# Sums of weight blocks for the second feed-forward network: formed in SBUF on the way to TensorE, in place of sums kept in HBM

## The chip, the cores and the metric

One core of one Trainium2 chip. The time is device microseconds (us) of one execution. Before the change the kernel takes 1630.29 us, the median of 3 runs (1623.0 to 1633.59). The engines are TensorE (PE; its weight load is PEld), VectorE (DVE), ScalarE (ACT), GpSimd (POOL) and SyncE (SP), which only issues transfers. All five run their own instruction streams in program order and meet at semaphores.

## The reference, cut to what matters

One layer of a decoder for 512 prompt tokens and 32 new tokens (544 columns), model width 1024:

```python
h = h + 0.5 * _swiglu(_rms(h, g_ffn1), w_ffn1_gate, w_ffn1_up, w_ffn1_down)
mix, ... = _mixer(_rms(h, g_mix), ...)       # S5 branch and latent attention branch
h = h + mix
h = h + 0.5 * _swiglu(_rms(h, g_ffn2), w_ffn2_gate, w_ffn2_up, w_ffn2_down)
y = _rms(h, g_final)

def _swiglu(x, w_gate, w_up, w_down):        # gate, up: 1024 x 2816; down: 2816 x 1024
    return (silu(x @ w_gate) * (x @ w_up)) @ w_down
```

All inputs are float32. The change is in how the weights of the second `_swiglu` reach TensorE.

## The kernel before, in words

**Precision.** Each float32 operand is split in a high part (fp32r, a rounding, by ScalarE) and a low part (the rest, a subtraction, by VectorE). A product is three matmuls: hi x hi, hi x lo, lo x hi. So every weight block passes ScalarE and then VectorE before TensorE may use it.

**Order of the work.** First FFN (22 blocks of 128 hidden columns in groups of 6, 6, 6 and 4; per group 12 or 8 gate and up tiles of 48 matmuls, then 8 down tiles with 6 or 4 chunks, so 36 or 24 matmuls); then the projections of the mixer with the S5 scan; attention; output; the second FFN. In the first FFN `split_hi` (L750, ScalarE: w_hi<-raw) and `split_lo` (L1405, VectorE: w_lo<-raw,w_hi) run two tiles ahead of TensorE (`products`, L2126). GpSimd forms the hidden product (L1199, L1201), and between its groups the tables of the S5 branch (L1283 to L1317), which wait for VectorE's `s5_parameters`. Later GpSimd adds squares for the norms (`add_squares`, L1190: m_sum), clears hprev and multiplies ktrig (L1347). TensorE's column sums (L2140) wait for m_sum, and a product with ropesum (L2384) for ktrig.

**The second FFN** is computed by a scheme with seven products in place of eight for each 2 x 2 arrangement of blocks (Strassen and Winograd). A unit takes four blocks A11, A12, A21, A22 of a weight. For 20 of the 22 hidden blocks the gate and the up tile, each in two halves, are the four (a gate/up unit; blocks of 128 x 512); 12 units are of the down weight (128 x 384). The first two hidden blocks and the last part of the down weight are computed plainly. The seven products P1 to P7 of a unit have these weights: P1 A11, P2 A12, P4 A22, P5 S1 = A21 + A22, P6 S2 = A11 + S1, P7 S3 = A11 + A21, P3 S4 = A12 + S2. A product is 12 matmuls (gate/up) or 9 (down) of 272 columns, by `product` (L2233). `ORDER` interleaves neighbouring units: P1 n, P2 n, P3 n-1, P7 n, P6 n, P4 n-1, P5 n. `part_hi` (L864, ScalarE) and `part_lo` (L1514, VectorE) split the weight of product k+8 after product k (NWS = 8 places). In a gate/up unit ScalarE evacuates P1 (L923), P7 (L925), P6 (L927) and P3 (L929), VectorE P2, P5 and P4 (L1571, L1575, L1579); in a down unit VectorE adds all seven to h (L1548). TensorE's P5 waits for the evacuation of P6 (p6_out), its P3 and P4 for that of P5 (c22), since the banks are accumulated on.

**Where the sums come from.** S1 to S4 of all 32 units lie in HBM (s2_a, s2_d). They are made during the first FFN and the mixer: `weight_copies` (L808) lets ScalarE issue 36 copies from HBM to HBM, some after each down tile of the first FFN, right behind `split_hi` in its program. `weight_sums` lets GpSimd issue 36 transfers that add in HBM, in three steps (L1245, then L1239, then L1234), each behind a wait for the step before. Its six calls stand between the pieces of GpSimd's work named above, two of them behind `add_squares(N_Q)` and `add_squares(N_KV)`; the third stands ahead of the hprev clearing and `add_squares(N_Q)`, and the fourth ahead of ktrig. In the second FFN SyncE loads one block per product, P1 to P7 of each unit (L736, a ring of 11 places wr).

**The hidden product** of a pair of blocks has seven combinations for the down units. GpSimd multiplies silu and up (L1262) and forms four sums (L1270, L1272 to L1274: hv<-hv). ScalarE (`hidden_hi`, L878 and L879: h_hi) and VectorE (`hidden_lo`, L1536: h_lo) split them after the product k in `READY`: for seven pairs that is a P3 of a gate/up unit, for two a P4 of a down unit.

## Time and profile before

| | us |
|---|---|
| median of 3 runs | 1630.29 |
| profiled execution, time | 1638.77 |
| its span | 1636.8 |
| PE busy (82%) | 1345.1 |
| DVE busy (46%) | 759.1 |
| ACT busy (31%) | 508.7 |
| POOL busy (24%) | 389.8 |

The profile shows one execution. Lines as L808 are those of the kernel's code. Instructions that issue transfers aren't counted as busy; where a transfer's issue holds an engine, its next instruction has "issue" as the end of its idle time. ACTq, POOLq and SPq are the engines' sequencers. PEclk is the clock that TensorE was granted, as a share of 2.4 GHz (0.5 is the lower level, 1.2 GHz). The trace has the transfers of the second FFN as wr<-w_gu, wr<-s_a, wr<-s_d and wr<-w_d2a or w_d2b, the copies as s_a<-w_gu and s_d<-w_d2a or w_d2b on ACTq, and the additions on POOLq. In the stretch 1382 to 1444 us gate/up units run, in 1444.8 to 1476 us down units. A few matmul records can be missing.

### The profile page before, as it was taken

Reading aid. Unit: us, or ns where it says so; the run is one execution under the profiler, and the core shown is the slowest. Engines: PE = TensorE matmul, PEld = TensorE weight load, DVE = VectorE, ACT = ScalarE, POOL = GpSimd, SP = SyncE. Lnnn points to the kernel's source line nnn. Section 1 sums busy time; section 2 is a strip of 40 time slices with the busy share of each in tenths; the row PEclk is TensorE's granted clock in tenths of the full one; section 3 lists DMA queues with packets and bytes.
Section 4 is the critical chain, followed back from the end, with each engine's and each line's share of the span. In section 5 each row is a group of like instructions: output and inputs, shape, how many; then the busy total and the mean of one; then the engine's idle time right before and its main releaser. Section 6 shows DMA issues by size and latency. Waiting matters only on the chain.

```text
span 1636.8 us, 28404 instructions
## 1 busy us (share of the span) xinstructions
PE 1345.1 (82%) x11292; PEld 1235.8 (76%) x11292; DVE 759.1 (46%) x1301; ACT 508.7 (31%) x941; POOL 389.8 (24%) x401
## 2 busy tenths in 40 slices
PE   7965389747973884819489999998999699999998
PEld 7964389747973884819376777765999699999997
DVE  6322033402220232629153444454556877686774
ACT  5220032002210221201023333243334564655554
POOL 0216013602280111211135222220121231221202
PEclk9986689968986896859788999999999899999998
DMA  6222232446266534858467999997523356556541
GB/s 214 76 83 85 105 126 83 141 105 165 80 168 139 156 104 179 207 108 189 85 175 240 318 340 335 347 321 288 184 87 97 110 158 198 170 171 187 148 150 55
DMA packets 157799, 273.26 MB, mean 167 GB/s; under 512 B 42161, under 2 KB 65106, under 8 KB 155506
## 3 DMA queue, kind: packets, MB, share of 16 engines
q1 hardware_dynamic: 96802, 199.72, 37.2%
q0 software_dynamic: 41344, 34.84, 11.6%
q10 hardware_dynamic: 19536, 37.10, 6.0%
q8 instruction: 79, 1.29, 0.3%
q14 instruction: 38, 0.31, 0.1%
HBM read 261.69 MB, written 70.50 MB: 203 GB/s over the span
## 4 chain that ended last, share of the span: by engine, by line
PE 51%; issue 17%; ACTq 11%; DVE 6%; DMA 6%; POOL 4%; ACT 3%; SPq 1%; another core or an unknown queue 1%; DVEq 0%; POOLq 0%
PE d L2126 20%; ACTq L808 11%; PE d L2233 8%; PE e L2233 8%; PE e L2471 5%; DMA kv<-kv_src 2%; DMA s_a<-w_gu 2%; DVE w_lo L1405 2%; ACT w_hi L750 2%; PE e L2503 1%; DMA raw<-w_q 1%; PE e L2522 1%; PE d L2535 1%; POOL s_a L1245 1%; SPq L538 1%
## 5 line engine op out<-in xcount | busy, mean ns | idle before, releaser
L1405 DVE TENSOR_TENSOR w_lo<-raw,w_hi 128x1024 fp32r<-128x1024 f32 (+2 forms) x127 | 152.6, 1201 | 443.7 <-ACT w_hi L750 443.4
L2126 PE MATMUL d<-x_hi,w_hi 128*128 128x272 f32 x976 | 216.2, 304 | 129.3 <-DVE w_lo L1405 75.8
L2126 PEld LDWEIGHTS d<-x_hi,w_hi 128*128 128x128 f32 x976 | 163.5, 201 | 135.4 <-DVE w_lo L1405 78.5
L750 ACT CAST w_hi<-raw 128x1024 fp32r<-128x1024 f32 (+2 forms) x127 | 123.3, 971 | 450.2 <-issue 213.2
L2126 PE MATMUL d<-x_lo,w_hi 128*128 128x272 f32 x976 | 210.7, 299 | 0.0
L2126 PE MATMUL d<-x_hi,w_lo 128*128 128x272 f32 x976 | 210.6, 299 | 0.0
L1514 DVE TENSOR_TENSOR ws_lo<-wr,ws_hi 128x512 fp32r<-128x512 f32 (+1 forms) x224 | 158.8, 711 | 68.4 <-ACT ws_hi L864 66.2
L2126 PEld LDWEIGHTS d<-x_lo,w_hi 128*128 128x128 f32 x976 | 162.8, 200 | 0.0
L2126 PEld LDWEIGHTS d<-x_hi,w_lo 128*128 128x128 f32 x976 | 161.8, 200 | 0.0
L864 ACT CAST ws_hi<-wr 128x512 fp32r<-128x512 f32 (+1 forms) x224 | 129.8, 581 | 85.5 <-PE d L2233 44.5
L2126 PE MATMUL d<-hid_hi,w_hi 128*128 128x272 f32 x352 | 83.4, 322 | 67.2 <-DVE w_lo L1405 66.0
L2126 PEld LDWEIGHTS d<-hid_hi,w_hi 128*128 128x128 f32 x352 | 62.8, 215 | 72.1 <-DVE w_lo L1405 35.2
L1381 POOL DMA_INDIRECT kr<-kr_src,gidx x64 | 60.9, 952 | 176.1 <-PE e L2506 165.2
L1262 POOL TENSOR_TENSOR hv<-sl,upb 128x544 f32<-128x544 f32 x21 | 36.1, 1718 | 259.3 <-DVE upb L1579 195.1
L2233 PE MATMUL e<-x_hi,ws_hi 128*128 128x272 f32 x280 | 82.2, 293 | 13.2 <-DVE ws_lo L1514 6.9
L1199 POOL TENSOR_TENSOR hid<-silu,up 128x544 f32<-128x544 f32 x21 | 31.0, 1475 | 235.6 <-DVE up L1466 235.6
L2233 PE MATMUL e<-x_hi,ws_lo 128*128 128x272 f32 x280 | 82.0, 293 | 0.0
L2233 PE MATMUL d<-x_hi,ws_hi 128*128 128x272 f32 x280 | 81.8, 292 | 0.0
L2233 PE MATMUL d<-x_hi,ws_lo 128*128 128x272 f32 x280 | 81.8, 292 | 0.0
L2233 PE MATMUL e<-x_lo,ws_hi 128*128 128x272 f32 x280 | 81.6, 292 | 0.0
L2233 PE MATMUL d<-x_lo,ws_hi 128*128 128x272 f32 x280 | 81.5, 291 | 0.0
L2126 PE MATMUL d<-hid_lo,w_hi 128*128 128x272 f32 x352 | 79.3, 310 | 0.0
(435 smaller groups left out, 3176.7 us busy)
## 6 DMA issues: line engine op xcount, KB each, us to landing
kv<-kv_src SPq DMA_DIRECT2D x256, 256.0 KB
raw<-w_gu SPq DMA_DIRECT2D x47, 512.0 KB, 5.8
wr<-s_a SPq DMA_DIRECT2D x80, 256.0 KB, 2.8
raw<-w_post SPq DMA_DIRECT2D x34, 512.0 KB, 4.4
...
wr<-w_gu SPq DMA_DIRECT2D x60, 256.0 KB, 3.0
...
```

Source lines behind the costliest of these rows:

```text
L538: sp.dma_start(dst, src).then_inc(s, 16)
L750: nc.scalar.copy(w_hi[:, s % 2, 0:n, :], raw[:, raw_pos(s), 0:n, :]).then_inc(S.hi_done, 1)
L808: nc.scalar.dma_start(summed(kind, q, i0, i1), weight_block(kind, QUARTER[q], i0, i1)).then_inc(sem["cp%d" % g], 16)
L864: nc.scalar.copy(ws_hi[k % NWS][:, 0:n, :], wr[k % NWR][:, 0:n, :]).then_inc(S.w_hid, 1)
L1199: nc.gpsimd.tensor_tensor(hid[:, j, :], silu[:, j, :], up[:, j, :], ALU.mult).then_inc(S.hid_done, 1)
L1262: nc.gpsimd.tensor_tensor(hv[:, 1:3, :] if j % 2 else hv[:, 0:8:7, :], halves(sl[:, j % 2, :]), halves(upb[:, j % 2, :]), ALU.mult).then_i ...
L1381: nc.gpsimd.indirect_dma_start(kr[v % NKR][:, j, :], None, a["kr_src"], bass.IndirectOffsetOnAxis(ap=gidx32[:, n:n + 1].bitcast(U32), axis ...
L1405: nc.vector.tensor_tensor(w_lo[:, s % 2, 0:n, :], raw[:, raw_pos(s), 0:n, :], w_hi[:, s % 2, 0:n, :].bitcast(FP), ALU.subtract).then_inc(S ...
L1514: nc.vector.tensor_tensor(ws_lo[k % NWS][:, 0:n, :], wr[k % NWR][:, 0:n, :], ws_hi[k % NWS][:, 0:n, :].bitcast(FP), ALU.subtract).then_inc ...
L2126: ins = mm(out[:, b, :], w[:, pos, c0 + k, :], x[:, k, b * HALF:(b + 1) * HALF], start=first, stop=stop)
L2233: ins = mm(out, w[k % NWS][:, c, :], v, start=typ in ("P1", "P2", "P7") and c == 0 and w is ws_hi and v is xh, stop=c == steps(n) - 1 and ...
L2471: ins = mm(job_bank(k), w[:, s % 2, c0 + c, :], x[:, c, half], start=c == 0 and x is xh and w is w_hi, stop=c == nk - 1 and w is w_lo)
```

## The change

The sums no longer exist in HBM. `weight_copies`, `weight_sums`, s2_a and s2_d are gone, and with them SyncE's wait for sums3. SyncE loads four blocks per unit, A11, A12, A21 and A22, 128 loads for 224, in a ring of 8 places: four for even units and four for odd. The load of a block for unit n waits until its last reader in unit n-2 is done. The sums are made in place in the loaded blocks, one after the other, each after the split that reads the place has finished:

- GpSimd, for all units: A11 += A21 (S3, after P1's split), A21 += A22 (S1).
- For gate/up units VectorE, right after the low part of P7's and of P6's weight: A11 += A22 (S2), A11 += A12 (S4). For down units GpSimd makes these two.
- ScalarE's split of P7, P5, P6 and P3 waits for the sum it reads.

GpSimd's order in the second FFN is now: sums of unit n+1, then the product silu x up of unit n-1's block. The four sums of each pair of hidden blocks (`hidden_sums`) move to VectorE, after `part_lo` and ahead of `hidden_lo` at the places in `READY`; `hidden_hi` waits for them as before.

```diff
-    NWR, NWS = 11, 8
+    NWR, NWS = 8, 8
...
+    HELD = ("A11", "A12", "A21", "A22")
+    FROM = {"P1": "A11", "P2": "A12", "P7": "A11", "P6": "A11", "P3": "A11", "P4": "A22", "P5": "A21"}
+    READ = {"A11": (0, 0), "A12": (0, 1), "A22": (1, 1), "A21": (1, 0)}
...
+    def read_last(n, x):
+
+        if x == "A12":
+            return S.s4_sum, n + 1
+        return after("w_lod", AT[{"A11": "P3", "A22": "P4", "A21": "P5"}[x], n] + 1)
...
-        sp.wait_ge(S.sums3, 16 * sum(len(g) for g in GROUPS))
-        for k in range(NP + KC):
-            if 3 <= k < NWR:
-                sp.wait_ge(S.lo_done, S_FFN2 + (k - 3) // 2 + 1)
-            if k >= NWR:
-                sp.wait_ge(*after("w_lod", k - NWR + 1))
-            if k >= NP:
-                src, n = a["w_d2b"][k - NP, :, (BLOCKS[1] + BLOCKS[2]) * P:], NLAST
-            else:
-                typ, u_ = ORDER[k]
-                src, n = unit_source(u_, typ), steps(u_)
-            sp.dma_start(wr[k % NWR][:, 0:n, :], src.rearrange("p (c n) -> p c n", n=P)).then_inc(sem[WR_IN[k % NWR][0]], 16)
+        def weight_load(n, x):
+
+            if n >= 2:
+                sp.wait_ge(*read_last(n - 2, x))
+            elif held(n, x) >= 3:
+                sp.wait_ge(S.lo_done, S_FFN2 + (held(n, x) - 3) // 2 + 1)
+            sp.dma_start(wide(n, x), weight_block(n, *READ[x]).rearrange("p (c n) -> p c n", n=P)).then_inc(sem[WR_IN[held(n, x)][0]], 16)
+
+        when = {"A12": 4.5, "A21": 6.5, "A11": 9.5, "A22": 12.5}
+        for n in range(2):
+            for x in ("A11", "A12", "A21", "A22"):
+                weight_load(n, x)
+        for t, n, x in sorted((7 * n + when[x], n, x) for n in range(2, NU) for x in HELD):
+            weight_load(n, x)
+        for m in range(KC):
...
+            typ, n = ORDER[k]
+            x = FROM[typ]
+            if typ == "P6":
+                act.wait_ge(S.s2_sum, n + 1)
+            elif typ == "P3":
+                act.wait_ge(S.s4_sum, n + 1)
+            elif typ == "P7":
+                act.wait_ge(S.s3_sum, n + 1)
+            elif typ == "P5":
+                act.wait_ge(S.s1_sum, n + 1)
+            else:
+                act.wait_ge(*landed(n, x))
...
-        def weight_sums(step):
-
-            if 0 <= step - 2 < len(GROUPS):
-                pool.wait_ge(S.sums2, 16 * sum(len(g) for g in GROUPS[:step - 1]))
-                for kind, i0, i1 in GROUPS[step - 2]:
-                    pool.dma_start(long_rows(summed(kind, 4, i0, i1)), long_rows(summed(kind, 2, i0, i1)), accum_op=ALU.add,
-                                   max_dma_last_dim=8192).then_inc(S.sums3, 16)
-            if 0 <= step - 1 < len(GROUPS):
-                pool.wait_ge(S.sums1, 32 * sum(len(g) for g in GROUPS[:step]))
-                for kind, i0, i1 in GROUPS[step - 1]:
-                    pool.dma_start(long_rows(summed(kind, 2, i0, i1)), long_rows(summed(kind, 1, i0, i1)), accum_op=ALU.add,
-                                   max_dma_last_dim=8192).then_inc(S.sums2, 16)
-            if step < len(GROUPS):
-                pool.wait_ge(sem["cp%d" % step], 64 * len(GROUPS[step]))
-                for kind, i0, i1 in GROUPS[step]:
-                    for q, x in ADDED.items():
-                        pool.dma_start(summed(kind, q, i0, i1), weight_block(kind, x, i0, i1), accum_op=ALU.add,
-                                       max_dma_last_dim=8192).then_inc(S.sums1, 16)
...
+        def add_in_place(n, to, x, done):
+
+            pool.wait_ge(*landed(n, x))
+            nc.gpsimd.tensor_tensor(wide(n, to), wide(n, to), wide(n, x), ALU.add).then_inc(done, 1)
...
-                pool.wait_ge(*after("mul", j + 1))
-                if j == 0:
-                    pool.wait_ge(*after("x7l", 3))
-                if j % 2 == 0:
-                    nc.gpsimd.tensor_tensor(hv[:, 3, :], hv[:, 0, :], hv[:, 7, :], ALU.subtract)
-                else:
-                    link(nc.gpsimd.tensor_tensor(hv[:, 5, :], hv[:, 7, :], hv[:, 2, :], ALU.subtract))
-                    link(nc.gpsimd.tensor_tensor(hv[:, 4, :], hv[:, 5, :], hv[:, 0, :], ALU.subtract))
-                    nc.gpsimd.tensor_tensor(hv[:, 6, :], hv[:, 1, :], hv[:, 4, :], ALU.add).then_inc(S.hvt, 1)
-
-            for j in range(sum(BLOCKS) - 1):
-                hidden(j, None)
+
+            for n in range(-1, NU):
+                if n + 1 < NU:
+                    pool.wait_ge(*after("w_lod", AT["P1", n + 1] + 1))
+                    add_in_place(n + 1, "A11", "A21", S.s3_sum)
+                    pool.wait_ge(S.s3_sum, n + 2)
+                    add_in_place(n + 1, "A21", "A22", S.s1_sum)
+                    if dense(n + 1):
+                        pool.wait_ge(*after("w_lod", AT["P7", n + 1] + 1))
+                        add_in_place(n + 1, "A11", "A22", S.s2_sum)
+                        pool.wait_ge(*after("w_lod", AT["P6", n + 1] + 1))
+                        add_in_place(n + 1, "A11", "A12", S.s4_sum)
+                if n + 2 <= HEAD:
+                    hidden(n + 1)
+                if n >= 1 and not dense(n - 1):
+                    hidden(pair_of(n - 1))
...
+            if typ == "P7" and not dense(n):
+                add_in_place(n, "A22", k, S.s2_sum)
+            if typ == "P6" and not dense(n):
+                add_in_place(n, "A12", k, S.s4_sum)
+
+        def add_in_place(n, x, k, done):
+
+            dve.wait_ge(*after("w_lod", k + 1))
+            dve.wait_ge(*landed(n, x))
+            nc.vector.tensor_tensor(wide(n, "A11"), wide(n, "A11"), wide(n, x), ALU.add).then_inc(done, 1)
...
+        def hidden_sums(q):
+            dve.wait_ge(*after("mul", 2 * q + 2))
+            nc.vector.tensor_tensor(hv[:, 3, :], hv[:, 0, :], hv[:, 7, :], ALU.subtract)
+            link(nc.vector.tensor_tensor(hv[:, 5, :], hv[:, 7, :], hv[:, 2, :], ALU.subtract))
+            link(nc.vector.tensor_tensor(hv[:, 4, :], hv[:, 5, :], hv[:, 0, :], ALU.subtract))
+            nc.vector.tensor_tensor(hv[:, 6, :], hv[:, 1, :], hv[:, 4, :], ALU.add).then_inc(S.hvt, 1)
...
                 if k in READY:
+                    hidden_sums(READY[k])
                     hidden_lo(READY[k])
```

## Rows read from the trace of the kernel before

**Rows 1.** The page's part 2: TensorE's busy tenths in forty slices
```profile
PE   7965389747973884819489999998999699999998
```

**Rows 2.** Stretches: length; busy (count) PE, PEld, DVE, ACT, POOL; clock, DMA, GB/s
```profile
103.80:210.20 106.40, 42.67 (x242) 41.36 (x241) 19.50 (x50) 9.43 (x13) 27.69 (x86) 0.69 0.26 92
319.40:392.00 72.60, 30.75 (x194) 30.09 (x193) 9.07 (x9) 6.40 (x8) 10.76 (x7) 0.71 0.48 118
473.20:546.40 73.20, 30.78 (x170) 29.83 (x169) 9.91 (x11) 4.86 (x6) 14.17 (x12) 0.67 0.63 149
602.50:660.50 58.00, 24.12 (x116) 22.88 (x115) 14.23 (x17) 11.53 (x18) 6.98 (x6) 0.67 0.46 167
698.40:731.40 33.00, 0.09 (x2) 0.06 (x1) 3.92 (x7) 1.59 (x2) 4.97 (x5) 0.54 0.46 92
779.60:800.70 21.10, 0.04 (x2) 0.01 (x1) 4.36 (x6) 1.04 (x1) 3.24 (x2) 0.58 0.58 105
838.40:845.40 7.00, 0.17 (x2) 0.08 (x1) 0.61 (x1) 1.48 (x3) 0.75 (x1) 0.70 0.82 243
```

**Rows 3.** Chain that ended last: start us, length us, what
```profile
30.84 54.37 PE d L2126 x432
...
1292.81 3.06 PE e L2233 x12
1295.87 4.27 PE d L2233 x24
```

**Rows 4.** Line 808: ns min/median/max, first and last start
```profile
L808 ACTq DMA_DIRECT2D s_a<-w_gu x24: 1214/10982/26296, 92.6 to 649.1; - x24
```

**Rows 5.** Waits, 97 to 212 us: total us, times, longest
```profile
ACT w_hi L750 <- issue: 71.8, 4, 21.5
```

**Rows 6.** Instructions in order of time, GpSimd, 583 to 880 us
```profile
725.60 1.88 POOL L1245 DMA_DIRECT2D s_a<-w_gu  x1 [44.12 <-issue]
```

**Rows 7.** Waits, 700 to 800 and 800 to 872 us
```profile
PE e L2140 <- POOL m_sum L1190: 32.9, 1, 32.9
...
PE e L2384 <- POOL ktrig L1347: 21.1, 1, 21.1
```

**Rows 8.** Busy time by stretch: gate and up units, then down units
```profile
1382.00:1444.00 62.00, 62.00 (x496) 61.99 (x495) 43.88 (x67) 38.89 (x77) 15.18 (x12) 1.00 0.55 164
1444.80:1476.00 31.20, 31.20 (x251) 31.20 (x250) 26.32 (x54) 14.59 (x28) 6.94 (x6) 1.00 0.66 196
```

**Rows 9.** Groups of instructions by shape, 1250 to 1637 us; busy us, mean ns
```profile
L1514 DVE TENSOR_TENSOR ws_lo<-wr,ws_hi 128x512 fp32r<-128x512 f32 x140 | 104.9, 753 | 51.7 <-ACT ws_hi L864 49.6
L1514 DVE TENSOR_TENSOR ws_lo<-wr,ws_hi 128x384 fp32r<-128x384 f32 x84 | 53.9, 641 | 16.7 <-ACT ws_hi L864 16.6
...
L1579 DVE TENSOR_TENSOR upb<-d,upb 128x272 f32<-128x272 f32 x10 | 4.4, 435 | 1.0 <-PE d L2233 1.0
...
L1262 POOL TENSOR_TENSOR hv<-sl,upb 128x544 f32<-128x544 f32 x21 | 36.1, 1718 | 259.3 <-DVE upb L1579 195.1 <-issue 42.0 <-DVE upb L1587 22.3
L1270 POOL TENSOR_TENSOR hv<-hv 128x272 f32<-128x272 f32 x9 | 9.7, 1076 | 10.7 <-DVE x_lo L1521 10.1
```

**Rows 10.** In order of time, ScalarE, around one P3 of the second FFN
```profile
1417.76 0.40 ACT L929 ACTIVATE sl<-e 128x272 f32<-128x272 f32 x1 [0.81 <-PE e L2233]
...
1418.57 0.88 ACT L878 CAST h_hi<-hv 128x816 fp32r<-128x816 f32 x1
1419.34 1.10 ACT L879 CAST h_hi<-hv 128x1088 fp32r<-128x1088 f32 x1
...
1421.47 0.38 ACT L927 COPY upb<-d 128x272 f32<-128x272 f32 x1
```

**Rows 11.** DMA issues: count, KB each, median us to landing
```profile
wr<-w_gu SPq DMA_DIRECT2D x60, 256.0 KB, 3.0
```

**Rows 12.** In order of time, VectorE: alone, then beside GpSimd
```profile
1423.43 0.68 DVE L1514 TENSOR_TENSOR ws_lo<-wr,ws_hi 128x512 fp32r<-128x512 f32 x1
...
1424.54 1.34 DVE L1514 TENSOR_TENSOR ws_lo<-wr,ws_hi 128x512 fp32r<-128x512 f32 x1
```

More of the change, by code:

```diff
@@ L328, in tile_of, with weight_block, held, wide @@
         return j if b + 1 == NB else j0 + (j - j0) // 2 + nb // 2 * ((j - j0) % 2)
-    SUMMED = [t for t in range(sum(BLOCKS)) if t not in [tile_of(j) for j in range(HEAD)]]
-    assert SUMMED == [1, 2] + list(range(4, 22)) and BLOCKS == (6, 6, 6, 4)
-    DB = KC // 2
-    GROUPS = ((("g", 0, 2), ("g", 2, 4), ("g", 4, 8)), (("d", 0, 4), ("g", 8, 12)), (("d", 4, 8), ("g", 12, 16)), (("d", 8, 12), ("g", 16, 20)))
-    QUARTER = {1: 2, 2: 0, 3: 0, 4: 1}
-    ADDED = {1: 3, 3: 2}
-    def weight_block(kind, x, i0, i1):
-        row, half = divmod(x, 2)
+    HELD = ("A11", "A12", "A21", "A22")
+    FROM = {"P1": "A11", "P2": "A12", "P7": "A11", "P6": "A11", "P3": "A11", "P4": "A22", "P5": "A21"}
+    READ = {"A11": (0, 0), "A12": (0, 1), "A22": (1, 1), "A21": (1, 0)}
+    def weight_block(n, row, half):
+        kind, where = UNITS2[n]
         if kind == "g":
-            t0, t1 = SUMMED[i0], SUMMED[i1 - 1] + 1
-            assert t1 - t0 == i1 - i0
-            return a["w_gu2"][2 * t0 + row:2 * t1 + row - 1:2, :, half * KC // 2 * P:(half + 1) * KC // 2 * P]
-        b, i = divmod(i0, DB)
+            return a["w_gu2"][2 * tile_of(where) + row][:, half * KC // 2 * P:(half + 1) * KC // 2 * P]
+        b, i = where
         w = BLOCKS[0] // 2 * P
         src, c = (a["w_d2a"], half * w) if b == 0 else (a["w_d2b"], (2 * (b - 1) + half) * w)
-        i1 -= b * DB
-        return src[2 * i + row:2 * i1 + row - 1:2, :, c:c + w]
-    def summed(kind, q, i0, i1):
-        return (s2_a if kind == "g" else s2_d)[q - 1, i0:i1]
-    def unit_source(n, typ):
-        x, kind = SOURCE[typ], UNITS2[n][0]
-        i = SUMMED.index(tile_of(pair_of(n))) if kind == "g" else DB * pair_of(n)[0] + pair_of(n)[1]
-        return (weight_block(kind, x, i, i + 1) if x < 4 else summed(kind, x - 3, i, i + 1))[0]
+        return src[2 * i + row][:, c:c + w]
+    def held(n, x):
+        return NWR // 2 * (n % 2) + HELD.index(x)
+    def wide(n, x):
+        return wr[held(n, x)][:, 0:steps(n), :]
+    def landed(n, x):
+        name, first = WR_IN[held(n, x)]
+        return sem[name], first + 16 * (n // 2 + 1)
+    def last_held(m):
+        i = (NWR // 2 * (NU % 2) + m) % NWR
+        n = NU + (i // (NWR // 2) != NU % 2)
+        return i, n, HELD[i % (NWR // 2)]
     def dense(n):
@@ L512, in build @@
                  trig_done uk_in hprev_zero gp_out0 gp_out1 gp_evac cqs_done qn_done zn_done gate_done merged_done mh_done m_ready fin_diag fin_rep gain_done y_dve dve_own pool_own
-                 cp0 cp1 cp2 cp3 sums1 sums2 sums3 p6_out p7_out""".split())
+                 s1_sum s3_sum s2_sum s4_sum p6_out p7_out""".split())
     sem = {n: nc.alloc_semaphore(n) for n in sem_names}
@@ L528, in build @@
              [("x_in%d" % i, 16) for i in range(4)] +
-             [("raw_in%d" % i, 16 * raw_count(S_FFN2 + i)) for i in range(NRAW)])
+             [("raw_in%d" % i, 16 * raw_count(S_FFN2 + i)) for i in range(NWR - NKV - 4)])
     S = type("Sems", (), sem)
@@ L802, in last_down @@
             last_root(1)
-        def weight_copies(g, m):
-            copies = [(kind, q, i0, i1) for kind, i0, i1 in GROUPS[g] for q in (1, 3, 2, 4)]
-            for kind, q, i0, i1 in copies[m * len(copies) // KC:(m + 1) * len(copies) // KC]:
-                nc.scalar.dma_start(summed(kind, q, i0, i1), weight_block(kind, QUARTER[q], i0, i1)).then_inc(sem["cp%d" % g], 16)
         def ffn(norm, g_next, norm_next):
@@ L862, in part_hi @@
                 act.wait_ge(S.tile_done, T_FFN2 + 3 + (k >= 6))
-            n = steps(ORDER[k][1])
-            nc.scalar.copy(ws_hi[k % NWS][:, 0:n, :], wr[k % NWR][:, 0:n, :]).then_inc(S.w_hid, 1)
+            nc.scalar.copy(ws_hi[k % NWS][:, 0:steps(n), :], wide(n, x)).then_inc(S.w_hid, 1)
         def x7_split_hi(i):
```

33 lines of the change are left out of this document (11 added, 22 removed).

## The prediction

> **What bounds the kernel now.** I read the page's forty slices first. TensorE is busy in nine tenths or more of nearly all slices from the twenty-second on (860 us), but in one to five tenths of several before, as in the fourth, fifth and eighteenth [rows 1]. So the span has two parts with different limits. I then cut the first part at the places where TensorE stands still. Seven stretches come out [rows 2]: together 371.3 us long, with only 728 matmuls in them. The price of one matmul without a stall is 54.37/432 = 0.126 us [rows 3], so these stretches hold 728 x 0.126 = 92 us of TensorE work and 279 us of something else. The granted clock in them is 0.54 to 0.71, a mixture of the 1.2 and the 2.4 GHz level.
>
> What is the something else? In the first stretch ScalarE's weight split (w_hi, L750) waits 71.8 us for "issue", that is, for its own queue [rows 5]. What stands in that queue is L808: each copy of a weight block from HBM to HBM holds ScalarE for a median of 10.98 us, up to 26.3 us, though nothing is computed [rows 4]. VectorE's half of the split waits for ScalarE's, TensorE for VectorE's. Stretches two to four have the same shape. Stretches five and six are GpSimd's: it issues the accumulating transfers (L1245) and is idle 44.12 us ahead of one [rows 6]; behind it in program order stand the additions m_sum and the product ktrig, for which TensorE waits 32.9 and 21.1 us [rows 7]. The seventh (7 us) is a late load of w_q, at a DMA share of 0.82 [rows 2].
>
> The second FFN, from about 1265 us, is the other kind: 62.00 of 62.00 us busy where gate and up units run, 31.20 of 31.20 where down units run, clock 1.00 [rows 8]. TensorE is the bound there and nothing can be gained; whatever the change adds there is either hidden or lost.
>
> **The change, part by part.**
>
> *1. Removed: 36 copies on ScalarE, 36 accumulating transfers on GpSimd.* What each stretch gives back is its length less its matmuls at 0.126 us [rows 2, 3]: 106.4 - 30.5 = 76; 72.6 - 24.4 = 48; 73.2 - 21.4 = 52; 58.0 - 14.6 = 43; 33.0; 21.1; 7.0 (7 at most). I don't take all of it, since something else is late next. In stretch four ScalarE and VectorE each have some 2.9 us of their own work per tile (w, x, h, square) against 24 x 0.126 = 3.0 us of TensorE, and the last x_lo, then m_sum, come one after the other: I leave 5 us there. In stretch five VectorE would still have its scan work, which now hides in the wait: 3 us left. One us each stays in six and seven. The S5 tables on GpSimd and VectorE, and the loads, run at another time than now but fit beside the tiles: GpSimd is busy 27.7 us of the 106 in the first stretch, mostly with the tables, and its next product is due only after four down and two gate/up tiles, 240 matmuls or 30 us of TensorE. Sum: 76 + 48 + 52 + 38 + 30 + 20 + 6 = 270 us.
>
> *2. Clock restarts.* After a gap the matmuls start at the lower level: twelve took 3.06 us after the gap at 1288 to 1293 us, where 1.51 would be full pace, and the next 24 took 4.27 us for 3.02 [rows 3]. That is 2.8 us behind one gap. The work behind six of the seven stretches starts so, outside the windows; at about 2 us each: 12 us. Parts 1 and 2: **282 us** less, bounds 230 (clock and half of what I left at nothing stay) and 295.
>
> *3. SyncE.* 224 loads become 128 of the same size; there is no wait for sums3, which is over long before. A load takes 3.0 us to land [rows 11]. The tightest block, A11, is free again after P3's split and wanted five products later, at least 5 x 9 x 0.126 = 5.7 us. Cost nothing; if transfers took twice as long, the first product of a unit would wait some 1 us, 30 times.
>
> *4. Additions in SBUF.* GpSimd gets 2 for each of 20 gate/up units and 4 for each of 12 down units, VectorE 2 for each of the 20. Nothing in the trace is this very instruction; the nearest are VectorE's two-input subtractions of the same size, 0.753 us (512) and 0.641 (384), and GpSimd's 1.718 us for 544 columns [rows 9]. So VectorE's addition is about 0.75 and GpSimd's about 1.6 us for 512 and 1.2 for 384; as bounds 0.68 to 1.34 (the same subtraction took 1.34 us beside GpSimd [rows 12]). GpSimd's load is 40 x 1.6 + 48 x 1.2 = 122 us over 306: it has the room. VectorE: 43.88/62 of a 10.6 us unit is 7.5 us now; plus 2 x 0.75, plus the moved sums (4 x 0.435 per two units [rows 9]) makes 9.9 of 10.6. It fits, with 7% to spare.
>
> GpSimd against VectorE: in 272 columns the trace has 1.076 against 0.435 us [rows 9]. The Trainium skill, *GPSIMD Engine Reference*, § 4.1 Engine selection, speaks against this part of the change: it gives elementwise work on a tile to VectorE, GpSimd being about twice as slow with two inputs; § 1 adds that the two share an SBUF interface. By that rule the 88 additions would go to VectorE, 40 x 0.75 + 48 x 0.64 = 61 us more of its time, which its 7% to spare doesn't hold; by the rows they lie beside TensorE's work on GpSimd, and only the slowdown of VectorE costs. The ratio agrees (2.5 here), the advice does not follow for an engine with nothing else to do.
>
> *5. The new waits.* The splits now hang on the additions: P7's on GpSimd's, P6's and P3's on one behind the previous split. They run eight products ahead, which absorbs that. But ScalarE and VectorE run in order, and behind a waiting split stands the evacuation of the product that TensorE needs soon: P5 waits for p6_out, one product after P6. In a down unit P6's split waits for a subtraction (0.56), GpSimd's sum (1.2) and then takes 1.1 itself: p6_out comes some 0.5 to 1 us late. Nine such units: 7 us. In a gate unit VectorE makes the sum in 0.75 us and the slack holds.
>
> *6. The sums of the hidden product* (36 instructions, four per pair) go from GpSimd to VectorE, behind the split and its addition. Now, in one such place, ScalarE starts h_hi at 1418.57, 0.8 us after P3 is done, because the sums were ready; it ends at 1420.4, and p6_out (L927) is written at 1421.8 [rows 10]. P5 could start at 1417.7 + 3 x 1.51 = 1422.2: 0.4 us of slack. In the new order VectorE finishes P7's subtraction about 1.7 us after P3, the addition at 2.4, the four sums at 2.4 + 4 x 0.45 = 4.2; only then h_hi (1.9), p7_out, P6's split, silu and p6_out (1.5): 7.6 us after P3, where 4.5 was free. **3.1 us of stall, seven times = 22 us**; the two pairs whose sums come behind a down unit's P4 lose about 2 us each through c22 (4 us). A gap of 3 us also brings the clock down (2.8 us by [rows 3] for a 5 us gap, nothing if the gap is too short): at 1.5 each, 13 us. Between ends of 0 (the waits overlap something) and 9 x 6 = 54 I take 39.
>
> *7. Start of the second FFN:* VectorE is the bound of those 25 us; two additions and one wait more: 4 us.
>
> Loss in the second FFN: 7 + 39 + 4 = **50 us**, bounds 10 and 110. The sum is against the profiled execution (span 1636.8, time 1638.77 us): 1638.8 - 282 + 50 = 1407. The median of the three runs is 8.5 us below that execution; taken off, 1398. I say **1400 us**.
>
> **Rivals.** (a) *The second FFN hides everything*: for it speaks that splits run eight products ahead; against it the 0.4 us of slack. 1630 - 282 + 0 to 10 = 1350. Chance 0.14.
> (b) *VectorE becomes the second FFN's bound*: 9.9 of 10.6 us on average leaves no room for contention; if every subtraction and addition takes the 0.95 us that lies between 0.68 and 1.34, a gate unit takes 7 x 0.25 + 2 x 0.25 = 2.2 us more, so 12.1 for 10.6, and a down unit 26.32/31.20 x 7.9 = 6.7 now, plus 7 x 0.2 of contention and 1.4 of waiting, 9.5 for 7.9: 20 x 1.5 + 12 x 1.6 = 49 us, on top of parts 6 and 7: about 1445 to 1490. For it: the 1.34 us row. Against: GpSimd loses 4 us of its own sums per pair. Chance 0.14.
> (c) *GpSimd's stretches stay*: the chain behind m_sum and ktrig is VectorE's scan and not the transfers, and stretches four to seven keep their length. Only 76 + 48 + 52 + 6 = 182 come back: 1630 - 182 + 50 = 1498. Against it: GpSimd was idle for 44 us with "issue" in front. Chance 0.07.
> (d) *Slower than before*: the stalls of the second FFN come so regularly that TensorE stays at 1.2 GHz there. 2436 matmuls at 0.255 us (3.06/12) take 621 us for 307: +314, against -282: 1630 - 282 + 314 = 1662. It decides against the change only if the clock is below 307/(307 + 282) = 0.52 through the whole FFN; the worst stretch now, with gaps of 5 to 15 us, has 0.54. Chance 0.02.
> (e) *The change doesn't do what it says*, the first part being slowed by something that stays: near 1630 plus the loss or minus a little. Chance 0.02.
>
> **The numbers.** The forecast has 0.61 with its own range 1365 to 1450. Taking in (a) at 1350 and the near part of (b) gives 1345 to 1470, with about 0.2 outside. One per cent, 16 us, is about what a measurement of this kernel tells from no change. Faster by over 1%: all but (d) and (e), 0.96; within 1%: 0.02; slower: 0.02.
>
> **What would show it.** In the profile after: no L808 and no L1245; the second FFN's products starting some 280 us earlier; ScalarE's "issue" wait ahead of w_hi gone; no TensorE gap over 5 us between there and the start. In the second FFN: seven gaps near 3 us in front of P5 (ScalarE h_hi waiting for VectorE's hv), two of 2 us in front of P3; GpSimd busy 150 us or more. The prediction is wrong if TensorE has no such gaps (a), if VectorE is at 95% there and TensorE's gaps are spread over all units (b), or if the m_sum wait stays above 10 us (c).

## The result: 1402 us for 1630, and the profile after

The changed kernel takes 1402.0 us (median of 4 runs, 1395.5 to 1408.2), the kernel before 1630.1 (1623.0 to 1633.6): ratio 0.8605, 95% interval [0.8557, 0.8654]. The forecast was 1400, range 1345 to 1470. The profiled execution of the changed kernel has a span of 1399.8 us.

The page of the profile after, part 2, answers to [rows 1]: TensorE's busy tenths and its granted clock, each slice now 35 us.

```profile
PE   7999999999999999999999989997698888898987
...
PEclk9999999999999999999999999999799999999999
```

The first part of the span has no slice below nine after the first; the holes have moved behind slice 28. The view by stretch shows both ends. Cut at the column sums of the norms, after (from, to, length; busy us and count of PE, PEld, DVE, ACT, POOL; clock, DMA share, GB/s):

```profile
22.00:435.20 413.20, 408.31 (x3519) 403.64 (x3518) 172.12 (x235) 117.83 (x148) 160.04 (x192) 1.00 0.28 87
435.20:471.00 35.80, 35.80 (x372) 34.92 (x373) 27.61 (x37) 8.21 (x10) 3.70 (x3) 1.00 0.35 116
471.00:540.20 69.20, 68.68 (x859) 63.25 (x858) 55.43 (x103) 13.58 (x17) 6.17 (x2) 1.00 0.24 75
540.20:946.00 405.80, 396.46 (x3650) 310.78 (x3650) 207.45 (x446) 146.28 (x341) 100.50 (x95) 1.00 0.73 256
946.00:1399.80 453.80, 379.93 (x2813) 373.35 (x2812) 354.58 (x541) 207.14 (x404) 153.79 (x121) 0.93 0.23 74
```

and the last two of these stretches before the change:

```profile
826.00:1250.40 424.40, 406.52 (x3651) 318.25 (x3650) 207.93 (x446) 146.58 (x341) 101.20 (x97) 0.97 0.75 258
1250.40:1636.80 386.40, 360.81 (x2813) 358.77 (x2812) 282.14 (x465) 209.74 (x404) 81.92 (x69) 0.97 0.48 145
```

Before, the third cut stood at 826.0; now it stands at 540.2: 286 us came back. In the attention part (fourth row) 18.6 us came back: 9.8 by the first ukt product, which is the seventh stretch of [rows 2] and its restart; the rest is the clock (1.00 for 0.97) in code that the change doesn't touch. The second feed-forward network (FFN) gave 67.4 us away, 453.8 for 386.4. Length less busy time is TensorE's idle time: 73.9 for 25.6, so 48.3 us more; its busy time is 19.1 us more, since matmuls behind a gap run at the lower clock. 286 + 18.6 - 67.4 = 237 = 1636.8 - 1399.8.

What the idle time waited for: the waits of the changed kernel, 990 to 1372 us (engine line, awaited: total us, times, longest).

```profile
ACT h_hi L892 <- DVE hv L1539: 28.5, 9, 3.5
ACT ws_hi L878 <- POOL wr L1239: 22.3, 9, 3.0
...
PE d L2243 <- ACT upb L941: 18.1, 7, 3.3
```

The first row has nine waits of ScalarE's h_hi for the moved sums; behind seven of them TensorE's P5 waits for p6_out (L941, third row). The second row is ScalarE's weight split waiting for GpSimd's sums. One such place in order of time (start, us, ..., idle before), the answer to [rows 10]; ScalarE:

```profile
1026.88 0.40 ACT L943 ACTIVATE sl<-e 128x272 f32<-128x272 f32 x1 [0.81 <-PE e L2243]
1027.18 0.61 ACT L878 CAST ws_hi<-wr 128x512 fp32r<-128x512 f32 x1
1031.00 0.87 ACT L892 CAST h_hi<-hv 128x816 fp32r<-128x816 f32 x1 [3.21 <-DVE hv L1539]
1031.78 1.09 ACT L893 CAST h_hi<-hv 128x1088 fp32r<-128x1088 f32 x1
1032.78 0.38 ACT L939 COPY upb<-d 128x272 f32<-128x272 f32 x1
1033.05 0.62 ACT L878 CAST ws_hi<-wr 128x512 fp32r<-128x512 f32 x1
1033.57 0.43 ACT L905 ACTIVATE sl<-sl 128x272 f32<-128x272 f32 x1
1033.90 0.37 ACT L941 COPY upb<-d 128x272 f32<-128x272 f32 x1
```

VectorE:

```profile
1023.09 1.21 DVE L1506 TENSOR_TENSOR ws_lo<-wr,ws_hi 128x512 fp32r<-128x512 f32 x1 [0.25 <-ACT ws_hi L878]
1024.87 1.34 DVE L1506 TENSOR_TENSOR ws_lo<-wr,ws_hi 128x512 fp32r<-128x512 f32 x1 [0.57 <-ACT ws_hi L878]
1026.13 0.42 DVE L1580 TENSOR_TENSOR sl<-sl,d 128x272 f32<-128x272 f32 x1
1026.48 2.10 DVE L1506 TENSOR_TENSOR ws_lo<-wr,ws_hi 128x512 fp32r<-128x512 f32 x2
1028.62 0.69 DVE L1517 TENSOR_TENSOR wr<-wr,wr 128x512 f32<-128x512 f32 x1
1029.23 0.43 DVE L1536 TENSOR_TENSOR hv<-hv 128x272 f32<-128x272 f32 x1
```

and TensorE's P5, after 3.05 us:

```profile
1034.42 0.36 PE L2243 MATMUL d<-x_hi,ws_hi 128*128 128x272 f32 x1 [3.05 <-ACT upb L941]
```

This is the chain that the prediction wrote out: split, addition, four sums, h_hi, p7_out, P6's split, silu, p6_out. Two of the four subtractions of weights (L1506) among VectorE's rows took 1.21 and 1.34 us, where one alone takes 0.68; both lie beside GpSimd's two-input instructions. The groups of instructions after, which answer to [rows 9]:

```profile
L1506 DVE TENSOR_TENSOR ws_lo<-wr,ws_hi 128x512 fp32r<-128x512 f32 (+1 forms) x224 | 193.6, 868 | 53.0 <-ACT ws_hi L878 51.3
L1239 POOL TENSOR_TENSOR wr<-wr,wr 128x384 f32<-128x384 f32 (+1 forms) x88 | 110.7, 1259 | 163.5 <-DVE ws_lo L1506 155.3
```

VectorE's subtractions (L1506) take 868 ns in the mean, where the kernel before had 711.

### The profile page after: what moved, and what is told of

Read it like the earlier page. It is cut to its first block, busy times and chain, and to the rows that moved or that the text cites. A ratio compares the mean times of both kernels' runs of the same rounds, so it can differ in the third digit from the quotient of the medians.

```text
span 1399.8 us, 28490 instructions
## 1 busy us (share of the span) xinstructions
PE 1303.8 (93%) x11292; PEld 1200.2 (86%) x11292; DVE 829.8 (59%) x1377; ACT 507.0 (36%) x941; POOL 424.5 (30%) x417
## 4 chain that ended last, share of the span: by engine, by line
PE 70%; DVE 10%; issue 6%; DMA 4%; POOL 4%; ACT 3%; SPq 1%; ACTq 0%; POOLq 0%; DVEq 0%
PE d L2136 36%; PE d L2243 7%; PE e L2243 7%; PE e L2481 6%; DMA kv<-kv_src 3%; DVE ws_lo L1506 2%; POOL wr L1239 2%; PE e L2513 2%; DVE w_lo L1397 2%; PE e L2532 1%; PE d L2545 1%; SPq L541 1%; ACT ws_hi L878 1%; PE e L2516 1%; PE d L2566 1%
## 5 line engine op out<-in xcount | busy, mean ns | idle before, releaser
L1506 DVE TENSOR_TENSOR ws_lo<-wr,ws_hi 128x512 fp32r<-128x512 f32 (+1 forms) x224 | 193.6, 868 | 53.0 <-ACT ws_hi L878 51.3
L2136 PE MATMUL d<-x_hi,w_hi 128*128 128x272 f32 x976 | 205.2, 292 | 10.5 <-DVE w_lo L1743 6.8
L2136 PE MATMUL d<-x_lo,w_hi 128*128 128x272 f32 x976 | 202.4, 289 | 0.0
L2136 PEld LDWEIGHTS d<-x_hi,w_hi 128*128 128x128 f32 x976 | 154.7, 190 | 13.2 <-DVE w_lo L1743 6.8
L1239 POOL TENSOR_TENSOR wr<-wr,wr 128x384 f32<-128x384 f32 (+1 forms) x88 | 110.7, 1259 | 163.5 <-DVE ws_lo L1506 155.3
L2136 PEld LDWEIGHTS d<-x_lo,w_hi 128*128 128x128 f32 x976 | 154.6, 190 | 0.0
L2136 PEld LDWEIGHTS d<-x_hi,w_lo 128*128 128x128 f32 x976 | 153.6, 190 | 0.0
L2136 PE MATMUL d<-hid_hi,w_hi 128*128 128x272 f32 x352 | 74.4, 292 | 4.1 <-DVE w_lo L1397 2.7
L2243 PEld LDWEIGHTS e<-x_hi,ws_hi 128*128 128x128 f32 x280 | 57.2, 204 | 22.9 <-DVE ws_lo L1506 16.3
L2243 PEld LDWEIGHTS d<-x_hi,ws_hi 128*128 128x128 f32 x280 | 56.0, 200 | 22.7 <-issue 22.7
```

The source lines that it names most:

```text
L1239: nc.gpsimd.tensor_tensor(wide(n, to), wide(n, to), wide(n, x), ALU.add).then_inc(done, 1)
L1506: nc.vector.tensor_tensor(ws_lo[k % NWS][:, 0:steps(n), :], wide(n, FROM[typ]), ws_hi[k % NWS][:, 0:steps(n), :].bitcast(FP), ALU.subtract ...
L2136: ins = mm(out[:, b, :], w[:, pos, c0 + k, :], x[:, k, b * HALF:(b + 1) * HALF], start=first, stop=stop)
L2243: ins = mm(out, w[k % NWS][:, c, :], v, start=typ in ("P1", "P2", "P7") and c == 0 and w is ws_hi and v is xh, stop=c == steps(n) - 1 and ...
```

## The experiments

Theory at the start (**order**): TensorE's gaps come from what stands in program order ahead of p6_out on ScalarE and VectorE; move it, and they go. Rival (**work**): VectorE has too much to do, by number of instructions or because GpSimd's additions stretch them. For each kernel the second FFN is cut as above, from its column sums to the end:

| kernel | time, us | ratio to before, 95% | FFN 2 | PE idle | PE busy | DVE busy |
|---|---|---|---|---|---|---|
| before | 1630.1 | 1 | 386.4 | 25.6 | 360.8 | 282.1 |
| f_none | 1341.6 | 0.8205 [0.8172, 0.8239] | 386.7 | 25.4 | 361.3 | 282.4 |
| f_copies | 1509.7 | 0.9238 [0.9201, 0.9275] | 386.3 | 25.4 | 360.9 | 282.3 |
| changed kernel | 1402.0 | 0.8605 [0.8557, 0.8654] | 453.8 | 73.9 | 379.9 | 354.6 |
| s_gpsimd | 1399.4 | 0.8569 [0.8534, 0.8605] | 440.6 | 68.5 | 372.1 | 344.5 |
| d_vector | 1404.6 | 0.8590 [0.8556, 0.8625] | 447.0 | 69.4 | 377.6 | 362.8 |
| s_early2 | 1394.3 | 0.8538 [0.8511, 0.8565] | 436.7 | 65.5 | 371.2 | 362.1 |
| s_early | 1393.9 | 0.8535 [0.8510, 0.8560] | 436.3 | 63.5 | 372.8 | 357.8 |
| d_defer | 1400.8 | 0.8584 [0.8557, 0.8611] | 444.4 | 66.8 | 377.6 | 358.9 |
| c_both2 | 1380.4 | 0.8460 [0.8435, 0.8485] | 428.3 | 52.5 | 375.8 | 358.1 |
| h_later | 1387.4 | 0.8487 [0.8466, 0.8508] | 429.2 | 54.6 | 374.6 | 361.1 |
| x_gp_small | 1379.8 | 0.8447 [0.8419, 0.8475] | 426.9 | 53.8 | 373.1 | 313.3 |
| v_only | 1402.1 | 0.8587 [0.8564, 0.8611] | 442.2 | 67.6 | 374.7 | 359.0 |
| v_all2 | 1364.8 | 0.8369 [0.8349, 0.8390] | 410.5 | 41.8 | 368.7 | 357.7 |

The stretches are those of one profiled execution each; PE idle varies least, since the clock's part falls differently from one execution to the next.

**f_none: the transfers out, nothing put in.** In the kernel before:

```diff
-                    weight_copies(b, m)
...
-        weight_sums(3)      # and the five other calls
...
-        sp.wait_ge(S.sums3, 16 * sum(len(g) for g in GROUPS))
...
-        return (weight_block(kind, x, i, i + 1) if x < 4 else summed(kind, x - 3, i, i + 1))[0]
+        return weight_block(kind, x % 4, i, i + 1)[0]
```

> The kernel before without the 36 copies and the 36 accumulating transfers, and without SyncE's wait for them; every one of the 224 loads of the second FFN takes an unsummed weight block of the same size, so the sums are left out and all else stays. Theory: the part ahead of the second FFN gives back what the changed kernel gave back there, 305 us by its traces, and the second FFN keeps its old length: 1630 - 305 = 1325 us (1315 to 1335), the second FFN's column sums at about 946 us, as in the changed kernel. By my forecast's own sum it would be 1630 - 282 = 1348. Rival (c), GpSimd's stretches belong to VectorE's scan: 1630 - 182 = 1448. Rival: part of the 305 us comes from the fewer loads of the changed kernel (128 for 224): above 1335.

Measured 1341.6 us. By stretch:

```profile
22.00:435.10 413.10, 408.32 (x3516) 403.45 (x3515) 172.54 (x235) 117.89 (x148) 159.73 (x191) 1.00 0.29 87
...
540.10:954.60 414.50, 402.04 (x3650) 314.53 (x3649) 207.56 (x446) 146.40 (x341) 100.59 (x95) 0.98 0.72 250
954.60:1341.30 386.70, 361.29 (x2814) 359.13 (x2812) 282.38 (x465) 209.74 (x404) 82.28 (x69) 0.97 0.48 145
```

The cuts lie where the changed kernel has them, within 0.1 us up to 540, and the second FFN has its old length. So the two halves of the change add up, and the number of loads (224 or 128) is nothing. The theory's range (1315 to 1335) was missed by 7 us, and above 1335 stood the rival that fewer loads gave a part. It isn't needed: f_none's attention part (414.5 us, with 224 loads still to come) lies in the middle of those of the ten experiments with 128. The whole gain of the front, by the ratio, is 0.1795 x 1634.6 = 293 us (288 to 299): more than the 282 of the forecast, less than the 305 that the two profiled executions show, because attention took 405.8 us in the one and 424.4 in the other; the twelve experiments have 409.5 to 419.0.

**f_copies: only GpSimd's transfers out.** As f_none, but `weight_copies` stays.

> The kernel before with ScalarE's 36 copies but without GpSimd's 36 accumulating transfers (the additions are left out; SyncE waits for the copies). Theory: the first three stretches stay, 76 + 48 + 52 = 176 us and their restarts; stretches five and six (30 + 20) and part of four (0 to 38) go, about 60 to 90 us: 1540 to 1570 us, the m_sum and ktrig waits of 32.9 and 21.1 us under 2 us. Rival: the copies are slow because the accumulating transfers fill the same DMA engines: then the copies' 10.98 us falls to under 6 us, the first three stretches shrink by half or more and the time is below 1480. Rival (c): 1620 or more, the two waits stay.

Measured 1509.7 us, below the theory's range and above the rival's. Waits over the whole execution, and the copies' line (ns min/median/max, first and last start), which answers to [rows 4]:

```profile
ACT w_hi L751 <- issue: 125.0, 11, 21.5
```

```profile
L809 ACTq DMA_DIRECT2D s_a<-w_gu x24: 1218/10137/16855, 92.5 to 587.2; - x24
```

The waits for m_sum and ktrig are gone, so rival (c) is out. The copies still hold ScalarE for 10.1 us at the median (10.98 before), but 16.9 at most, not 26.3; ScalarE's wait, 125.0 us in 11 times, was 213.2 us in 14 times before. The mixer's column sums start at 600.1 us: 62 us of what the prediction gave to the copies alone in stretches one to four came from copies that ran beside the accumulating transfers; 165 us (600.1 - 435.1) are the copies' own. The first stretch is unchanged, the second and third shrank.

**s_gpsimd: the sums of the pair back on GpSimd**, behind its product (the four instructions move from `hidden_sums` to `hidden`).

> The changed kernel with one part undone: the four sums of each hidden pair are GpSimd's again, right behind its product, ahead of its additions for the next unit. Theory (what counts is what stands in order in front of ScalarE's p6_out): h_hi no longer waits for VectorE, but GpSimd's additions come 4.3 us later and P7's split waits for S3 in its place, by some 2 us; the gaps shrink from 3.0 to about 2, nine times, 1385 to 1400 us. Rival (VectorE's amount of work is the bound, 2.6% of its time taken away): the gaps of the gate units go and also those of the down units get smaller, 1365 to 1380 us. Rival (the move cost nothing): 1402, gaps as now.

1399.4 us: no gain that the intervals tell. The nine gaps of 3 us went, but there are 17 gaps of 0.6 to 1.8 us now, two of 3.3, and the three of 2.5 to 2.8 at the transitions from down to gate units stay. The time lies at the upper end of the theory's range; the count of gaps fits neither theory.

**d_vector: S2 and S4 of the down units on VectorE.**

> The changed kernel with S2 and S4 of the 12 down units on VectorE, as in the gate/up units (24 additions of 384 columns moved from GpSimd). Theory: in a down unit P6's split waits for a subtraction and a sum; VectorE's sum takes about 0.6 us where GpSimd's takes 1.01 and has a semaphore more, so p6_out comes 0.5 us earlier and the seven gaps of 1.1 to 1.75 us shrink by about 0.5 each, 3 to 5 us in all: 1397 us. Rival (VectorE's amount of work is the bound): 24 x 0.6 us = 14 us more of its time makes gaps in the down units grow, 1405 to 1420 us.

1404.6 us, the same: above the theory's 1397, just under the rival's 1405. In the profile the down units' gaps (all of 0.4 us and more) fell from 11.0 to 6.3 us in all, close to what order says, and the time doesn't show it.

**s_early2 and s_early: the four sums two products, or one, ahead.**

```diff
+                if k + 2 in READY:          # s_early: k + 1
+                    hidden_sums(READY[k + 2])
                 if k in READY:
-                    hidden_sums(READY[k])
                     hidden_lo(READY[k])
```

> The changed kernel with VectorE's four sums of a hidden pair two products earlier in its program (behind the split after P1 in place of P3; for two pairs P7 in place of P4), where VectorE still had idle time; ScalarE's h_hi stays. Theory (order in front of p6_out): the nine gaps of 2.6 to 3.3 us fall under 0.6 us, 26 us, and with them some 12 us at the lower clock; the gaps of the down units stay. The second FFN, 453.8 us in the changed kernel from its column sums to the end, gets 415 to 422 us long: time 1402 - 35 = 1367 us (1360 to 1378). Rival (VectorE's amount of work is the bound): the work is the same, so the gaps move to the products ahead (P2, P3) and the time stays within 1395 to 1405.

> As the last, but one product earlier only (behind the split after P2; P6 for the two of P4). There VectorE works without a break, so the sums end 1.9 us earlier because the split of P7 and its addition now come behind them. Theory: the nine gaps of 3.0 us shrink by 1.9 to about 1.1, 17 us, and most of the clock's part goes: 1372 to 1385 us. Rival (amount of work): 1395 to 1405.

1394.3 and 1393.9: 8 us, at the edge of what the intervals tell, where 35 and 25 were expected. The order theory failed in its size. Nine gaps of 3 us became gaps of 0.9 to 1.8 in nearly every unit. VectorE works without a break from 1033 to 1040 us there, and the sums themselves are stretched: in s_early2, in order of time,

```profile
1032.67 1.62 POOL L1239 TENSOR_TENSOR wr<-wr,wr 128x512 f32<-128x512 f32 x1
1033.07 1.53 DVE L1536 TENSOR_TENSOR hv<-hv 128x272 f32<-128x272 f32 x1
```

0.43 us of work takes 1.53 beside GpSimd's addition.

**d_defer: P6's split behind the evacuation of the P6 before it.**

```diff
+    def one_later(part, k):
+        late = lambda i: i < NP and ORDER[i][0] == "P6"
+        if late(k + NWS - 1):
+            part(k + NWS - 1)
+        if not late(k + NWS):
+            part(k + NWS)
...
-                part_hi(k + NWS)            # part_lo the same
+                one_later(part_hi, k)
```

> The changed kernel with one step of ScalarE's and VectorE's order changed: the split of a P6 (high and low part, with VectorE's addition behind it) comes one product later in their programs, behind the evacuation of the P6 before it in place of ahead of it. Theory: the seven gaps of 1.1 to 1.8 us in the down units (10 us) and the three of 2.5 to 2.8 us where a down unit is followed by a gate/up unit (8 us) go, and the seven in front of P5 shrink by the split and the wait for its sum, 1.2 to 1.5 each (9 us); with 5 to 10 us of clock the second FFN gets 415 to 425 us long: 1366 us (1360 to 1382). Rival (amount of work): no gain in the down units, 1390 or more. Rival (the split of P6 gets late itself, since it has seven products of lead in place of eight): P6's own start shows a new gap.

1400.8 us, the same as the changed kernel. The down units' gaps went (0.7 to 0.9 left) and those of the three transitions fell from 2.5 to 2.8 to 1.7 or 1.8, but the nine others took 29 us in all for 26.5: four of them are 2.5 to 2.8 us long now, five 3.3 to 4.1. Why, in order of time:

```profile
1024.87 0.43 DVE L1596 TENSOR_TENSOR upb<-d,upb 128x272 f32<-128x272 f32 x1
...
1025.54 1.61 POOL L1263 TENSOR_TENSOR hv<-sl,upb 128x544 f32<-128x544 f32 x1 [5.27 <-DVE upb L1596]
...
1027.24 0.39 ACT L945 COPY sl<-d 128x272 f32<-128x272 f32 x1 [2.30 <-PE d L2251]
...
1034.36 0.87 ACT L900 CAST h_hi<-hv 128x816 fp32r<-128x816 f32 x1 [4.62 <-DVE hv L1547]
```

TensorE stands still from 1033.25 (37.26 less 4.01), so by five products of 1.51 us P1 was done at 1025.7 and P4 at 1022.7. P4's evacuation (L1596) comes 2.2 us after that, behind P6's low half and its sum, where it came 0.7 us after in the changed kernel. It starts GpSimd's product, which ends at 1027.15; ScalarE's evacuation of P1 (L945) waits for the product and begins at 1027.24, 1.5 us late (the row names the matmul; in h_later, at the same instruction, it names the product). The splits and sums behind it are late by as much. There is a ring: P4's evacuation, the product, P1's evacuation. A microsecond moved out of one arc of it is put into another.

**c_both2: s_early2 and d_defer together.**

> Both edits together: the sums two products earlier and the split of P6 one product later. Theory: nothing of the change's cost is left in the second FFN but its start, 392 to 400 us for the stretch (386.5 before the change): 1345 us (1338 to 1352). Rival: the two gains overlap and VectorE's amount of work keeps 10 to 20 us, 1355 to 1365.

1380.4 us: 22 us better than the changed kernel, more than the two parts (8 and 1), less than half of what order promised (57).

**x_gp_small: GpSimd's additions cut to 16 columns**, in the changed kernel, so the rest of those sums is left out. This is the direct test of the stretching.

> The changed kernel with each of GpSimd's 88 additions cut to 16 of its columns (the rest of those sums is left out); every wait and every other instruction stays. The last four kernels moved order alone and gained half of what the order theory said. Theory now (VectorE's amount of work beside GpSimd's): VectorE's split subtractions take 868 ns in the mean in the changed kernel and 711 before, so GpSimd's additions stretch them; without them the mean is about 710, VectorE gets some 30 us back, P6's split of a down unit no longer waits for GpSimd's sum, and the second FFN, 453.8 us, gets 425 to 435 us long; the three gaps of the sums of a pair in front of P5 stay at about 2 us. Time 1377 us (1370 to 1388). Rival (order alone, stretching costs nothing): only the seven short gaps of the down units go, 444 us, time 1392 to 1402.

1379.8 us and 426.9 for the stretch, as expected. The groups:

```profile
L1506 DVE TENSOR_TENSOR ws_lo<-wr,ws_hi 128x512 fp32r<-128x512 f32 (+1 forms) x224 | 150.2, 672 | 66.3 <-ACT ws_hi L878 65.2
...
L1239 POOL TENSOR_TENSOR wr<-wr,wr 128x16 f32<-128x16 f32 x88 | 25.4, 288 | 195.5 <-DVE ws_lo L1506 169.6 <-DMA wr<-w_gu 17.8 <-DMA wr<-w_d2b 4.7
```

The same 224 subtractions take 150.2 us, 43 us less than beside whole additions, and VectorE's busy time falls by 354.6 - 313.3 = 41.3 us. Of the seven gaps in front of P5 four are still 3.03 to 3.06 us long: that chain is order alone, as the prediction priced it. The three next to the down units fell from 2.8 to 2.0, and the down units' own went. The expectation has three gaps of about 2 us there; that four stay at 3 us it didn't foresee. VectorE's 41 us are shown; how the 22 us of time divide isn't, since the sums themselves also end sooner: ScalarE's wait for them (L1239) fell from 22.3 to 8.9 us, and that relief is the down units'.

**h_later: h_hi and h_lo two products later**, with d_defer.

> P6's split one product late, and the hidden pair's split h_hi and h_lo two products later (behind the evacuation of the P6 that TensorE's P5 waits for; the four sums stay where the change put them). No work less on VectorE. If order is what is left (nothing long stands in front of p6_out any more, VectorE's mean load is 9.9 us of 10.6): the gaps fall under 1 us, second FFN 405 to 418 us, time 1365 us (1357 to 1374). If VectorE's amount of work is what is left: as with both edits of order, 1378 to 1385. If h_lo now comes too late for the first product of the down units: three gaps of 1 us or more there, where TensorE waits for h_lo.

1387.4 us, 7 more than c_both2, not 1365. The third case came, and the time lies 2 us above the range of the second: h_lo (2.2 us) now stands ahead of the evacuations of P4, which is in the ring above, and of P5 (L1592), for which TensorE waits; and the first product of the down units waits for h_lo. TensorE's waits in it:

```profile
PE d L2252 <- DVE upb L1592: 8.7, 5, 2.6
...
PE e L2252 <- DVE h_lo L1553: 7.0, 3, 2.5
```

**v_all2 and v_only: every weight sum on VectorE**, GpSimd makes none; v_all2 on c_both2, v_only on the changed kernel.

```diff
+            if typ == "P1":
+                add_in_place(n, "A21", k, S.s3_sum)
+            if typ == "P2":
+                # wait for s3_sum and A22, then A21 += A22 on VectorE, s1_sum
...
-            if typ == "P7" and not dense(n):
+            if typ == "P7":
...
-            if typ == "P6" and not dense(n):
+            if typ == "P6":
```

> The kernel with both edits of order (sums of the pair two products early, P6's split one product late: 1380.4 us, second FFN 428.3 us), and all four weight sums of every unit on VectorE: 88 additions more there, none on GpSimd. Counting from rows: a gate/up unit in which a pair is finished has 7 x 0.69 + 4 x 0.69 + 3 x 0.43 + 4 x 0.44 + 2.2 = 12.8 us of VectorE in 10.6, its neighbour 8.9, a down unit 7 x 0.56 + 4 x 0.56 + 7 x 0.43 = 9.2 in 7.9. Theory (VectorE's amount of work): 12 x 1.3 = 16 us more from the down units, the gate units as now since GpSimd no longer stretches them: 1395 us (1388 to 1405). Rival (GpSimd's stretching and lateness cost more than its work saves, so the additions belong to VectorE): 1380 or less.

> The changed kernel with one edit: all four weight sums of every unit on VectorE, in the order of the changed kernel otherwise (no edit of order). It closes the square of four: changed kernel (453.8 us of second FFN), both edits of order (428.3), both and the sums on VectorE (410.5), and this. Theory (GpSimd's additions cost the second FFN through the stretching of VectorE's instructions and through their own lateness, whatever the order): the sums on VectorE gain as much as there, 18 us: 436 us (430 to 442), time 1384 us (1376 to 1392), the subtractions' mean near 700 ns, the seven gaps in front of P5 at 3 us as before, since their chain of VectorE instructions was not stretched. Rival (VectorE's load decides where P6's split stands ahead of p6_out: 61 us more work come on the path): 450 us or more, time 1398 or more. By my forecast's own weighing (GpSimd is the better place): above 1402.

v_all2 takes 1364.8 us, the fastest of the kernels that compute all of the sums and clearly faster than c_both2; the rival was right and my count wrong. There are 88 additions more on VectorE, 128 in all for 83.1 us by the rows below, and yet it is busy for 357.7 us where c_both2 has 358.1:

```profile
L1504 DVE TENSOR_TENSOR ws_lo<-wr,ws_hi 128x512 fp32r<-128x512 f32 (+1 forms) x224 | 155.5, 701 | 13.2 <-ACT ws_hi L886 11.1 <-PE d L2248 1.6
L1521 DVE TENSOR_TENSOR wr<-wr,wr 128x512 f32<-128x512 f32 (+1 forms) x96 | 62.7, 653 | 3.3
L1511 DVE TENSOR_TENSOR wr<-wr,wr 128x512 f32<-128x512 f32 (+1 forms) x32 | 20.4, 636 | 3.1 <-DMA wr<-w_d2b 1.6 <-DMA wr<-w_gu 1.0 <-DMA wr<-w_d2a 0.4
```

My count was also too high because a recorded instruction overlaps the next one. In v_all2, in order of time, down units:

```profile
1078.81 0.55 DVE L1504 TENSOR_TENSOR ws_lo<-wr,ws_hi 128x384 fp32r<-128x384 f32 x1
1079.28 0.43 DVE L1561 SCALAR_TENSOR_TENSOR h<-d,h 128x272 f32<-128x272 f32 x1
1079.63 0.55 DVE L1504 TENSOR_TENSOR ws_lo<-wr,ws_hi 128x384 fp32r<-128x384 f32 x1
```

0.55 and 0.43 us long, but 0.47 and 0.35 apart. A down unit is then 11 x 0.47 + 7 x 0.35 = 7.6 us, not 9.2; TensorE needs 7.9. The Trainium skill says this (*Perfetto Trace Analysis*, Optimizing Scalar/DVE Operations: the profiled latency holds a write part that overlaps the next instruction); the 0.08 us here agree.

v_only takes 1402.1: no gain, against the theory's 1384, though TensorE's idle time fell by 6.3 us and the subtractions' mean is 679 ns. Four of the seven gaps are 3.04 to 3.06 us again and three 2.6. So the edits of order and the sums on VectorE give more together than their sum: one by one 0 and 22 us, together 37. By the ratios it is 3, 24 and 38 us, and the intervals leave the 12 us between open by some 10. That the changed kernel's order hides what VectorE wins isn't shown: v_only takes GpSimd's additions away but puts them on VectorE, which stays as busy (359.0 us for 354.6), and x_gp_small, which puts nothing in their place, gained 22 us in that same order. The kernel with c_both2's order and short additions wasn't run.

## Why the prediction was right, and where its steps failed

The mechanism was right at both ends, and two terms off by 11 and 15 us cancelled: that the total came within 2 us is luck in part.

- **Parts 1 and 2 (282 us, bounds 230 and 295).** f_none gives 293. What I kept back behind stretches four to six (5, 3, 1 us) was not needed: nothing was late next, and the stretch of 35.8 us after the mixer's sums is 35.80 busy. The copies' share was mis-read in one respect: 62 us of the first four stretches needed both kinds of transfers.
- **Part 3 (loads, nothing).** Right; f_none loads 224 blocks and is not slower ahead, and in the changed kernel's second FFN no wait of TensorE is for a load.
- **Part 4, durations.** VectorE's addition 0.69 us (forecast 0.75). GpSimd's 88 took 110.7 us (forecast 122). Their effect was costed at nothing for VectorE: that failed. They took 41 us of VectorE's time. The kernel had this in [rows 12], and I used it as a bound and for rival (b) only. That VectorE's 7% to spare doesn't hold 61 us more also failed: the 88 additions take 55 us there (by v_all2's rows, 0.70 and 0.56 us each), and it holds them, because without GpSimd's additions beside them the subtractions take 155.5 us where c_both2 has 195.3. The Trainium skill's rule (*GPSIMD Engine Reference*, § 4.1 Engine selection: elementwise work on a tile belongs to VectorE) bore out, with 15.6 us, once the order was mended, and made no difference in the order of the change. The Trainium skill, *Perfetto Trace Analysis*, Optimizing Scalar/DVE Operations, is nearer to it: the two share a port, so moving work between them might not help. v_only and s_gpsimd agree with that, one each way.
- **Part 5 (down units 7 us; gate units nothing).** The seven gaps over 1 us of the down units sum to 10.0 us, by the forecast's chain: the one of 1.71 us ends at 1082.41 us, right behind VectorE's evacuation (L1557, at 1081.88), that behind a split which waited for ScalarE's, and ScalarE's waited 2.93 us for GpSimd's sum. "The slack holds" failed at the three places where the last down unit meets a gate unit: 2.50, 2.75 and 2.80 us, 8 us in all, since P6 of the down unit is evacuated by VectorE behind the gate unit's addition and split of 512 columns.
- **Part 6 (26 us of gaps, 13 of clock).** Nine gaps, 26.5 us, seven in front of P5 by p6_out and two by c22, each where the prediction had it. The clock cost more: busy time rose by 19.1 us over all gaps.
- **Part 7 (4 us).** 4.0 us: between the same two products of the start lie 31.3 us, 27.3 before.

Together 26.5 + 10.0 + 8.0 + 4.0 = 48.5 us of idle time (48.3 by the stretches) and 19.1 of clock: 67 for the forecast's 50. By the times it is (0.8605 - 0.8205) x 1630 = 65. Rival (b)'s stretching was there at about two thirds of its price (the subtractions of 512 columns took 881 ns where it had 950, and 753 before), but VectorE was busy for 78% of the second FFN, not 95.

What stays open: of the changed kernel's 60 to 65 us, v_all2 recovers 37 to 39; 24 us remain in its second FFN, 16 of them idle time of TensorE (41.8 less 25.4), some 3 at the start and the rest in gaps of up to 2.0 us. That the ring of P4, product and P1 carries these was read from rows and not tried by itself.
